# The low parts of the weights made in four operations over quarters, in a kernel of two hybrid transformer blocks

## The reference, cut to what matters

```
x = x + short_conv_mixer(rms_norm(x), w_in, conv_k, w_out)      # (b * causal_conv(c * u)) @ w_out
x = x + swiglu(rms_norm(x), w_gate, w_up, w_down)               # silu(h @ w_gate) * (h @ w_up) @ w_down
x = x + dilated_attention_mixer(rms_norm(x), w_qkv, w_out, rel_bias)   # 3 dilated branches, merged by their log-sums
x = x + swiglu(rms_norm(x), ...)
x = rms_norm(x)
x = x + ssd_mixer(rmsnorm(x), ...)    # state-space scan in both directions, 8 groups of 4 heads, chunks of 128
x = x + gla_mixer(rmsnorm(x), ...)    # gated linear attention in both directions, 4 heads, chunks of 64
x = rmsnorm(x)
```

## Time and profile before

| | us |
|---|---|
| median of 3 runs | 2196.06 |
| lowest and highest | 2195.3, 2196.64 |
| the profiled execution | 2197.22 |
| its span, first to last instruction | 2195.5 |
| PE busy | 2100.2 |
| DVE busy | 1005.7 |
| POOL busy | 957.5 |
| ACT busy | 784.8 |

### The profile page before, as it was taken

The page is one execution under the profiler, slowest core; times in us unless marked ns, Lnnn a source line. Parts: engine busy times, 40 slices in busy tenths (PEclk is TensorE's granted clock), DMA queues, the critical chain, the costliest instruction groups (busy, mean ns, idle before and its releaser), DMA issues.

```text
span 2195.5 us, 27013 instructions
## 1 busy us (share of the span) xinstructions
PE 2100.2 (96%) x10715; PEld 1713.2 (78%) x10715; DVE 1005.7 (46%) x1441; ACT 784.8 (36%) x1126; POOL 957.5 (44%) x403
## 2 busy tenths in 40 slices
PE   7999999999999989999999889999989989999898
PEld 5877888888777778888887778888868776766776
DVE  3184534332433444334324888878761254453321
ACT  3123222222344432222223445455542154353342
POOL 4434444444323224444443587878854421222132
PEclk9999999999999999999999989999989989999999
DMA  4223333233422213332233222222223221111221
GB/s 140 96 95 107 96 96 96 84 93 99 128 78 87 77 58 96 96 96 90 80 106 105 65 59 61 67 71 60 58 58 96 81 77 39 58 59 39 58 77 58
DMA packets 235403, 177.85 MB, mean 81 GB/s; under 512 B 9219, under 2 KB 231735, under 8 KB 235288
## 3 DMA queue, kind: packets, MB, share of 16 engines
q1 hardware_dynamic: 232256, 175.44, 26.4%
q10 hardware_dynamic: 3000, 0.72, 0.2%
q0 software_dynamic: 32, 0.07, 0.0%
HBM read 173.73 MB, written 2.47 MB: 80 GB/s over the span
## 4 chain that ended last, share of the span: by engine, by line
PE 42%; issue 32%; POOL 19%; DVE 5%; ACT 2%; POOLq 0%; DMA 0%; ACTq 0%; DVEq 0%
PE bank L1805 13%; PE bank L1806 12%; PE bank L1807 12%; POOL wlo L595 11%; POOL MT L621 2%; POOL P L618 2%; PE bank L2386 1%; POOL P L615 1%; POOL acc L615 1%; PE bank L2368 1%; POOL t L632 1%; DVE xc L1504 1%; POOL ybuf L641 1%; PE bank L2382 1%; POOL xw L632 1%
## 5 line engine op out<-in xcount | busy, mean ns | idle before, releaser
L595 POOL TENSOR_TENSOR wlo<-raw,whi 128x2048 fp32r<-128x2048 f32 (+1 forms) x168 | 736.2, 4382 | 1146.3 <-ACT whi L680 1141.1
L1805 PE MATMUL bank<-hHi,whi 128*128 128x512 f32 x1408 | 557.2, 396 | 7.8 <-DVE xc L1504 3.9
L1807 PE MATMUL bank<-hHi,wlo 128*128 128x512 f32 x1408 | 550.0, 391 | 0.0
L1806 PE MATMUL bank<-hLo,whi 128*128 128x512 f32 x1408 | 549.9, 391 | 0.0
L680 ACT ACTIVATE whi<-raw 128x2048 fp32r<-128x2048 f32 (+1 forms) x168 | 303.8, 1808 | 469.6 <-PE bank L1807 468.6
L1805 PEld LDWEIGHTS bank<-hHi,whi 128*128 128x128 f32 x1408 | 265.3, 188 | 77.6 <-issue 21.3
L1807 PEld LDWEIGHTS bank<-hHi,wlo 128*128 128x128 f32 x1408 | 265.2, 188 | 56.4
L1806 PEld LDWEIGHTS bank<-hLo,whi 128*128 128x128 f32 x1408 | 265.3, 188 | 54.5 <-issue 1.2
L1805 PE MATMUL bank<-whi,hHi 128*128 128x256 f32 x896 | 259.1, 289 | 5.9 <-ACT lg L1131 3.9
L1806 PE MATMUL bank<-wlo,hHi 128*128 128x256 f32 x896 | 255.2, 285 | 0.0
L1807 PE MATMUL bank<-whi,hLo 128*128 128x256 f32 x896 | 255.0, 285 | 0.0
(11 more groups left out here) (341 smaller groups left out, 3041.8 us busy)
## 6 DMA issues: line engine op xcount, KB each, us to landing
raw<-in_ssd_w_in SPq DMA_DIRECT2D x48, 512.0 KB, 4.6
raw<-in_ffn_w_gate SPq DMA_DIRECT2D x44, 512.0 KB, 4.6
raw<-in_ffn_w_up SPq DMA_DIRECT2D x44, 512.0 KB, 4.7
raw<-in_gla_w_in SPq DMA_DIRECT2D x40, 512.0 KB, 4.7
raw<-in_conv_w_in SPq DMA_DIRECT2D x24, 512.0 KB, 4.4
raw<-in_ffn_w_down SPq DMA_DIRECT2D x32, 384.0 KB, 3.4
raw<-in_attn_w_qkv SPq DMA_DIRECT2D x24, 512.0 KB, 4.3
raw<-in_ffn_w_down SPq DMA_DIRECT2D x32, 320.0 KB, 3.8
```

The lines of the kernel that those rows point to most:

```text
L595: pool.tensor_tensor(wlo[s][:, 0:w], raw[s][:, 0:w], whi[s][:, 0:w].bitcast(F32), ALU.subtract).then_inc(w_lo, 1)
L1805: pe.matmul(dst, hi1, hi2, start=first, stop=False)
L1806: pe.matmul(dst, hi1, lo2, start=False, stop=False)
L1807: return pe.matmul(dst, lo1, hi2, start=False, stop=last)
```

## The change

The one subtraction over the unit becomes four subtractions over quarters of its columns, 128x512 each (128x352 in a down projection), one after the other. Only the fourth signals `w_lo`, and only ahead of the first is there a wait. What is read, written and computed is the same, and so are all semaphore counts.

```diff
             def low(k, s, w=UNIT):
 
                 pool.wait_ge(w_hi, k)
-                pool.tensor_tensor(wlo[s][:, 0:w], raw[s][:, 0:w], whi[s][:, 0:w].bitcast(F32), ALU.subtract).then_inc(w_lo, 1)
+                for q in range(4):
+                    part = slice(w // 4 * q, w // 4 * (q + 1))
+                    ins = pool.tensor_tensor(wlo[s][:, part], raw[s][:, part], whi[s][:, part].bitcast(F32), ALU.subtract)
+                ins.then_inc(w_lo, 1)
```

## The result

The changed kernel takes 2184.66 us (median of 5 runs, 2183.45 to 2185.07), beside 2195.30 (2194.33 to 2196.64) for the kernel before on the same chip: 10.6 us less, ratio 0.9950, 95% interval 0.9936 to 0.9965. The forecast was 2190.9, -5.15 us, in a range that began at 2185.5.

The account below looks back on a forecast made before the run. PE, busy for 96% of the span, bounds the kernel, so only its waits counted: -1.3 + 1.3 - 2.0 + 0.5 - 1.85 - 1.8 = -5.15 us, giving 2190.9 us. The range was 2185.5 to 2199.5.

Parts of the forecast that it names:

- convolution: Short convolution, 127 to 170 us: DVE's chain gains from the seams and PE's waits there shrink, -1.3 us.
- attention output: PE's wait at 796.12: two DVE operations enter at seams and delay `wlo`, +1.3 us, all on PE.
- SSD entrance: From 1208 to 1281: DVE's chains freed earlier, `wlo` later, terms -0.5, -0.3 and -1.2, together -2.0 us.
- last group: Last SSD group, PE's wait at 1612.10 for the last `MT`, behind a POOL chain with one `wlo`: +0.5 us.
- GLA: DVE's stalls at 1792.37 and 1845 shortened by turns, -1.85 and -1.8 us of PE's waits; nothing at 1924.45.
- rival 2: The clock gives more: shorter waits, both in GLA, spare PE stretches at 1.2 GHz, some 4 us, 2187; 10%.
- It costs POOL 0.45 us: At each seam one waiting DVE operation goes in, lengthening POOL's work by 0.45 us.
- the turns: DVE operations entering at the three seams of a unit, 0.45 us of POOL time each.
- the matmuls behind it need this very `wlo`: GLA, 1924.45: L1770 gains 2.2 us, but PE must wait for that `wlo` anyway, so 0.
- rival 4: POOL's lateness decides at the entrances; ACT's next step takes back GLA's gain: +6.1 us, 2202; 13%.
- Quarters that do not let DVE in: DVE cannot enter between quarters, so nine places each pay +0.4 us: +3.6 us, 2199.7; 15%.
- POOL's lateness as the decider: Turns make `wlo` late at the entrances and GLA's gain is taken back: +6.1 us, 2202; 13%.

Follow-up runs that it names:

- e3: Kernel before, with quarters only in the last 35 units (rest of SSD's output projection, GLA), whole operations elsewhere; 2189.20 us.
- e4: Changed kernel, but each unit cut into one long operation and three of 32 columns, so all seams come at the end; 2195.03 us.
- e1: Kernel before, with quarters only in the 108 units of convolution, attention and the two FFNs, whole operations from SSD on; 2195.31 us.
- e2: Kernel before, with quarters only in 25 units, from the first SSD unit to the first of its output projection; 2191.42 us.
- e6: Changed kernel, but with eight operations a unit (256 columns, 176 in narrow units) instead of four; 2194.87 us.
- e10: Kernel before, with quarters in unit 114 only, whose low part starts at 1274.12; 2196.17 us.
- e7: Changed kernel, but with whole operations in the FFNs and the attention with its output projection; 2181.68 us, ratio 0.9929 to the kernel before.

## Why the prediction was wrong, and where it was right

The sum of the prediction was one of PE's waits alone. Place by place, from the first profile of each:

| place | wait before, after (us) | change | forecast |
|---|---|---|---|
| convolution, 157.29 and 169.75 | 0.26 and 1.18, none | -1.44 | -1.3 |
| attention output, 796.12 | 6.49, 7.83 | +1.34 | +1.3 |
| SSD entrance, 1212.73 to 1281.22 | 13.1, 10.1 | -3.0 | -2.0 |
| last group, 1599.86, 1606.58, 1612.10 | 6.4, 8.35 | +1.9 | +0.5 |
| GLA, 1798.91, 1852.07, 1856.41, 1928.76 | 12.0, 8.1 | -3.9 | -3.65 |
| sum | | -5.0 | -5.15 |

The sum of the waits came out as forecast; PE's idle time fell by 95.3 - 90.2 = 5.1 us in the first profiles and by 96.2 - 89.8 = 6.4 in the mean of both. The rest of the 10.6 us, 4 to 5.5, is in no wait. It is PE's busy time, 2098.5 in the mean of two profiles and 2091.7 after.

**The step that failed is the clock's term.** The sum priced every saved wait at its own length and PE's busy time at no change. The clock stood beside it as rival 2, "some 4 in all", at 10%, and not in the sum. What the runs showed in its place is 6.8 us less of busy time for the same matmuls. Of this, about 4 us are lost at the same places whichever profile of before is compared with whichever of the changed kernel. The table cuts the four profiles into windows of equal work, that is, with the same matmuls in each (length, and PE busy, in us; the order is before, before again, changed, changed again):

| place, times of before | length | PE busy |
|---|---|---|
| SSD entrance, 1190 to 1298 | 108.0, 107.8, 103.9, 102.2 | 93.5, 93.3, 92.1, 91.5 |
| last group, 1577 to 1645 | 68.0, 66.5, 66.9, 66.9 | 58.2, 55.1, 54.9, 55.0 |
| GLA, 1790 to 1870 | 80.0, 80.3, 77.3, 77.1 | 70.5, 70.3, 69.6, 69.8 |
| GLA, 1870 to 1980 | 110.0, 110.0, 107.9, 107.9 | 105.7, 105.7, 105.6, 105.7 |
| GLA, 1980 to 2110 | 130.0, 130.0, 128.4, 128.4 | 115.1, 115.1, 113.5, 113.5 |

The windows of SSD's entrance in the first profiles, with the granted clock (the third number from the end) at 0.91 and 0.95 of full speed:

```profile
1190.00:1298.00 108.00, 93.47 (x458) 74.58 (x458) 86.13 (x114) 49.14 (x78) 62.41 (x47) 0.91 0.22 64
```

```profile
1187.42:1291.36 103.94, 92.07 (x458) 73.14 (x458) 82.79 (x114) 49.12 (x78) 68.20 (x63) 0.95 0.23 67
```

GLA's start:

```profile
1790.00:1870.00 80.00, 70.52 (x414) 48.74 (x412) 42.53 (x64) 37.10 (x56) 13.57 (x3) 0.89 0.13 40
```

```profile
1782.75:1860.05 77.30, 69.63 (x414) 49.16 (x412) 38.91 (x64) 37.56 (x57) 15.19 (x12) 0.93 0.15 45
```

and the stretch from 1980 on:

```profile
1980.00:2110.00 130.00, 115.12 (x707) 89.11 (x704) 49.25 (x77) 53.40 (x87) 28.35 (x7) 0.93 0.17 49
```

```profile
1967.94:2096.29 128.35, 113.46 (x707) 88.60 (x704) 46.66 (x77) 53.40 (x87) 33.19 (x25) 0.95 0.17 50
```

PE's busy time is less by 1.2 to 2.0 us at SSD's entrance, by 0.5 to 0.9 at GLA's start and by 1.6 from 1980 on, whichever two profiles are compared: 3.3 to 4.5 together. In the last group the two profiles of before differ by 3.1 us between themselves, so nothing can be given to the change there. Rival 2 had the size, but not the place: it gave some 4 us to the two waits of GLA's start, which brought 0.5 to 0.9. From 1980 to 2110 PE's waits are the same before and after, and what is missing is one stretch at 1.2 GHz near 1999; which of the earlier differences spares it is not shown.

Two other numbers bear on it. In e3, PE is busy at the lower clock for 21.3 us from GLA's start to 2110, against 26.3 and 25.9 in before, which is 2.3 to 2.5 us of time; with the -3.9 us of its waits that makes -6.2 to -6.4, and its median fell by 6.3. And the mean granted clock is 0.982 or 0.983 in each of the five executions of the changed kernel, and 0.979 to 0.981 in each of the 64 executions of the kernel before beside the experiments. That mean cannot be turned into time, since it counts stretches in which PE waits as well: in e4 it is 0.980 to 0.985, and e4 gains nothing.

What stays open is how the rest is split. The single profiles of e1, e2 and e3 lose 0.3, 1.1 and 0.8 us of busy time (against 2098.5) and 0.6, 2.2 and 5.5 of idle time (against 96.2): 2.1 and 8.3, where the change has 6.8 and 6.4. The medians, -10.6 with an interval from -7.7 to -14.1, leave room for all of it.

**The seams.** Right: one waiting operation goes in at each, and DVE is freed after a quarter. PE's waits ahead of L2368 were to be 3.4 and 1.9 us and are 3.59 and 1.72. e4 shows that it is the seam's time that counts. "It costs POOL 0.45 us" holds for operations of 512 columns; the four L1706, of 128, cost 0.07 us together.

**POOL's time.** Four quarters in the quiet take 5.03 us (5.04 forecast), as here in the changed kernel:

```profile
1650.67 5.03 POOL L597 TENSOR_TENSOR wlo<-raw,whi 128x512 fp32r<-128x512 f32 x4 [5.85 <-ACT whi L683]
```

The busy time grew by 122.6 us, not 60 to 90: I had left the turns out there, at most 1.35 us a unit. It was hidden, as I said: PE waits for no `wlo` in the FFNs of the changed kernel, and e1 takes 2195.31 against 2195.48.

**Steps that were wrong in themselves.** At 1928.76 I had 0, since "the matmuls behind it need this very `wlo`". They do not: they use the unit before, and what they waited for is ACT's `lg`, whose line stood behind the stalled L1770. Before, and then after:

```profile
1856.41 0.35 PE L1805 MATMUL bank<-whi,hHi 128*128 128x256 f32 x1 [0.57 <-ACT lg L1131]
...
1928.76 0.35 PE L1805 MATMUL bank<-whi,hHi 128*128 128x256 f32 x1 [2.54 <-ACT lg L1131]
```

```profile
1844.97 0.35 PE L1808 MATMUL bank<-whi,hHi 128*128 128x256 f32 x1 [2.36 <-ACT lg L1134]
...
1916.70 0.35 PE L1808 MATMUL bank<-whi,hHi 128*128 128x256 f32 x1 [0.43 <-ACT lg L1134]
```

That gave 2.1 us that I had not, and at 1856.41 ACT's next step took back 1.8 us of GLA's gain, which I had given to rival 4 alone. The two nearly cancel, as do the deeper gain at SSD's entrance and the larger loss in the last group, where four quarters with turns in them stand ahead of `MT` (1600.22, a wait of 4.35 us for 0.08 before). So that the sums match (-5.0 and -5.15) owes something to luck.

**The rivals.** Quarters that do not let DVE in (15%) and POOL's lateness as the decider (13%) are out for four operations; for eight the second is a part of what happens (e6).

## What to carry to other kernels

Where GpSimd makes long two-operand SBUF operations beside VectorE, cut them in two or four: the first seam frees VectorE, and two give as much as four here. Keep them whole where TensorE waits for their very result, and look at each wait behind VectorE for what it would wait for next. Count a saved wait of TensorE with the slow stretch behind it: the sum of the waits gave half of the gain. To tell the two apart, compare TensorE's busy time over windows with the same matmuls in them, in more than one profile of each kernel.

## What the runs showed of the hardware

- A GpSimd operation of 512, 1024, 2048 columns: medians of all units are 1.29, 2.39 and 4.60 us; four quarters with nothing of VectorE between them take 5.03 us, so cutting costs some 0.14 us per seam.
- A VectorE operation that goes in at a seam lengthens the quarter beside it by some 0.45 us if it has 512 columns (1.72 and 1.74 us instead of 1.27, in e10 and e7), by 0.18 if it has 256 (1.45, in e10), and hardly if it has 128 (four of them and four quarters: 5.10 instead of 5.03 us).
- Three operations of 32 columns behind one of 1952 make 4.99 us; the median of all four kinds is 0.28 us, so a GpSimd operation of 32 columns takes about a quarter of a microsecond.
- For the same 10715 matmuls TensorE's busy time is 2089.9 to 2100.2 us in 14 profiles; less half of what it is busy at 1.2 GHz (44.6 to 66.2 us), it is 2065 to 2069.
- The same program, profiled twice, has its stretches at 1.2 GHz at the same places within a few us, but some are longer in the one or missing in the other, and PE's busy time differs by 3.5 us. The Trainium skill ("TensorE: Matmul & The Clock Gate", Part 1) says of the matmuls at a kernel's start that the same kernel can have more or fewer of them at the low clock from run to run; the 2100.2 and 2096.7 us agree, with stretches all through the kernel.
